# Two stacked transformer blocks on one core: ring slots, the order of splits and gates, and the PSUM banks of the last attentions rearranged

## The chip, the cores and the metric

The kernel runs on one core of a Trainium2 chip as one launch. The metric is the device time of that launch in microseconds (us), as the median of the runs shown. Times inside a run come from one execution that the hardware profiler recorded.

## The reference

The input `x` is 512 tokens of 1024 features in float32. Two blocks are computed one after the other. What matters of them, cut down:

```python
# block 1, two layers (l = 0, 1)
proj = h @ w_in[l]                         # q, k, v, gates of three kinds of attention
ya = differential_attention(...) * silu(ag)    # kind A: 4 heads, two maps each, rope on q and k
yb = forgetting_attention(...) * silu(bg)      # kind B: 4 heads
yc = stick_breaking_attention(...) * silu(cg)  # kind C: 4 heads
h = layernorm(ALPHA * h + concat(ya, yb, yc) @ w_out[l])
# block 2, one layer
proj = rms_norm(x) @ w_in_2
score = sum over 8 heads of relu(iq . ik) * iw # kind I; then the 128 largest of each row
o_a = attention over the chosen keys + bias    # kind X: 4 heads
o_b = hgrn2_mixer(q, f, i, g)                  # "hgrn": 4 heads, chunks of 64
o_c = mla_attention(...)                       # kind M: 4 heads
mixed = sigmoid(gates) * (o_a @ up_a, o_b @ up_b, o_c @ up_c), summed
x = x + mixed @ w_out_2
x = x + (silu(h @ w_ffn_gate) * (h @ w_ffn_up)) @ w_ffn_down
out = rms_norm(x)
```

## The kernel before, in words

A planner written in Python (`plan`, with `second` for block 2) makes one list of `steps`. Each of the five engines walks this same list and takes out of it what is its own, in order; semaphores join them. So the order of the list is the order in every engine's queue.

**Groups and split weights.** A `group` is one accumulation into one PSUM bank. The large ones multiply in three terms per slice of 128 features (x_high w_high, x_low w_high, x_high w_low), with K = 8 slices, so 24 matmuls for 512 columns. A weight piece (512 KB) is loaded by a transfer on SyncE's queue into a slot of the `raw` ring, ScalarE copies its rounded high part into a slot of the `high` ring (L1952), and GpSimd subtracts the high part from the raw piece in place (L1422). The step that does both is `split`; `place_splits` puts it behind the group that frees its slots (`free_raw`, `free_high`) and never ahead of the step named by `state["after"]`. The transfer of a piece waits for the last group that used what lay in its raw slot. The activations are split in the same way by `split_x`: ScalarE copies the high part (L1968), VectorE subtracts (L2422).

**Rings.** `RINGS_1` serves block 1 and the start of block 2 (7 raw slots, 7 high), `RINGS_FRONT` the projections around the I items (5 and 5), `RINGS_MIX` everything up to the end of the hgrn part (3 and 3), `RINGS_TAIL` the rest (9 and 9). A new ring starts again at its first slot. The plan's groups of block 1 and hgrn use three PSUM banks (`proj`) in turn; two banks hold scores, one the turned probabilities (`T`), two the outputs (`O[0]`, `O[1]`).

**Items.** An item is one head and one tile of 128 queries; it has K = 128 to 512 keys. `tick` emits one stage of each of several items: scores of item n, `soft1` of n, `soft2` of n-1, for kind C `soft3` of n-2, `trans` of n-3 (TensorE turns the probabilities into T, ScalarE copies T to SBUF, L1842), `pv` of n-4, and `fin` of a unit (all tiles of one head or pair) when its last item is 4 behind. For kind I the tick also emits two rounds of `topk` and one step of the list `tables` (20 entries: for each of four heads one `bias_rows` and four `bias` groups, the latter followed by two predicated copies on VectorE, L2122).

**Weaving.** In block 1 `weave` gives each projection job a weight; weight times a rate of the item kind is credit, and one tick is made per whole credit, for kinds B and C also in the middle of a group (a `half` step, then the rest). Before the output projection `wo` the groups of tiles 0 and 1 are begun on chunks 0 to 5 of y (`half`, `cut` = 6), then `flush` ticks the last items out, and the rest follows. In the hgrn part `paced` follows a written list of jobs per head: levels -1 to 5 (`hg_attn`), between them projections of the next head and `next_gate`, then `hg_turn`, `hg_state`, `hg_chain` (VectorE), `hg_out`, `hg_meansq`, `hg_norm`. `next_gate` emits `sig_min`, `sig_ln`, `sig_out` of earlier gates and one `sigmoid` group of 24 matmuls. ScalarE's copy of group i out of its bank (L1779) waits until the transfer of gate i-2 to DRAM has landed. There are 24 such gates; 22 come before the step `tail`, two behind it, and then the 24 `up` groups.

The `tail` step makes ScalarE wait for all scores, outputs and gates. `split_x` of y chunks writes into the buffer `hT_high`, which the projections read.

## Time and profile before

| | us |
|---|---|
| median of 3 runs | 1962.64 (1958.49 to 1964.73) |
| the profiled execution, time | 1960.21 |
| its span | 1958.4 |
| TensorE (PE) busy | 1747.6 |
| VectorE (DVE) busy | 866.7 |
| ScalarE (ACT) busy | 801.5 |
| GpSimd (POOL) busy | 590.6 |
| granted TensorE clock, mean | 0.94 |

Times in rows are us from the start of the span. In a row of a timeline the first number is the start, the second the duration of the merged instructions; in brackets stands how long the engine was idle before it and what ended that. A row of waits has the total, the number and the longest. A row of windows has the stretch, its length, then busy time and number of instructions of PE, PE's weight loads, DVE, ACT and POOL, then the granted TensorE clock (1.00 is 2.4 GHz, 0.50 is 1.2 GHz), the busy share of the DMA engines and GB/s. With a source line only that line's engine is counted. PE = TensorE, PEld its weight loads, SP = SyncE.

### The profile page before, as it was taken

Reading aid. Unit: us, or ns where it says so; the run is one execution under the profiler, and the core shown is the slowest. Engines: PE = TensorE matmul, PEld = TensorE weight load, DVE = VectorE, ACT = ScalarE, POOL = GpSimd, SP = SyncE. Lnnn points to the kernel's source line nnn. Section 1 sums busy time; section 2 is a strip of 40 time slices with the busy share of each in tenths; the row PEclk is TensorE's granted clock in tenths of the full one; section 3 lists DMA queues with packets and bytes.
Section 4 is the critical chain, followed back from the end, with each engine's and each line's share of the span. In section 5 each row is a group of like instructions: output and inputs, shape, how many; then the busy total and the mean of one; then the engine's idle time right before and its main releaser. Section 6 shows DMA issues by size and latency. Waiting matters only on the chain. (4 is left out here: it accounts for less than half of the span.)

```text
span 1958.4 us, 20995 instructions
## 1 busy us (share of the span) xinstructions
PE 1747.6 (89%) x7742; PEld 1325.8 (68%) x7742; DVE 866.7 (44%) x1478; ACT 801.5 (41%) x1512; POOL 590.6 (30%) x291
## 2 busy tenths in 40 slices
PE   4899998889999987898989898978779989999997
PEld 3666765567667655675655675767658778888786
DVE  4353344553533445452895656465417313211402
ACT  2244446522344465323324555555443334443411
POOL 4332222134322121322211222222046435444540
PEclk9998999899989998998989998989889989999999
DMA  6312212033122120323112222322155333333221
GB/s 179 92 44 65 65 44 65 12 86 87 46 65 57 51 75 12 87 81 87 32 46 65 60 70 60 113 60 74 39 168 187 86 95 97 97 96 99 77 97 43
DMA packets 204116, 149.85 MB, mean 77 GB/s; under 512 B 14956, under 2 KB 183536, under 8 KB 204016
## 3 DMA queue, kind: packets, MB, share of 16 engines
q1 hardware_dynamic: 199488, 133.57, 24.1%
q0 software_dynamic: 4528, 14.95, 2.4%
q8 instruction: 63, 1.03, 0.2%
q14 instruction: 37, 0.30, 0.0%
HBM read 138.00 MB, written 10.49 MB: 76 GB/s over the span
## 5 line engine op out<-in xcount | busy, mean ns | idle before, releaser
L1422 POOL TENSOR_TENSOR weights_rounded<-weights_raw,weights_rounded 128x1024 fp32r<-128x1024 f32 (+1 forms) x237 | 562.9, 2392 | 1153.1 <-ACT weights_rounded L1952 1152.8
L1488 PE MATMUL proj<-hT_high,weights_rounded 128*128 128x512 f32 (+1 forms) x1904 | 643.0, 409 | 35.7 <-POOL weights_rounded L1422 20.4
L1488 PEld LDWEIGHTS proj<-hT_high,weights_rounded 128*128 128x128 f32 x1904 | 370.1, 195 | 126.2 <-issue 39.0
L1488 PE MATMUL proj<-hT_low,weights_rounded 128*128 128x512 f32 (+1 forms) x952 | 379.1, 398 | 0.0
L1952 ACT ACTIVATE weights_rounded<-weights_raw 128x1024 fp32r<-128x1024 f32 (+1 forms) x237 | 233.6, 1009 | 140.2 <-DMA weights_raw<-in_w_ffn_down 58.7
L1484 PE MATMUL proj<-weights_rounded,hT_high 128*128 128x512 f32 (+1 forms) x640 | 209.3, 405 | 40.7 <-DVE hT_low L2033 15.8
L1488 PEld LDWEIGHTS proj<-hT_low,weights_rounded 128*128 128x128 f32 x952 | 185.7, 195 | 40.4 <-issue 5.3
L1484 PEld LDWEIGHTS proj<-weights_rounded,hT_high 128*128 128x128 f32 x640 | 125.9, 200 | 71.6 <-issue 32.2
L1611 PE MATMUL score<-qk 64*128 64x256 f32 (+3 forms) x256 | 79.6, 496 | 28.4 <-DVE logits L2201 15.2
L1654 PE MATMUL attn_out<-probs_T,V 128*64 128x128 f32 (+1 forms) x560 | 89.2, 294 | 0.0
L1640 PE MATMUL turned_probs<-constants,probs 128*128 128x128 f32 x320 | 61.0, 291 | 22.7 <-ACT probs_T L1842 22.5
L1654 PEld LDWEIGHTS attn_out<-probs_T,V 128*64 128x64 f32 (+1 forms) x560 | 69.6, 171 | 11.0 <-issue 9.3
L1484 PE MATMUL proj<-weights_rounded,hT_low 128*128 128x512 f32 (+1 forms) x192 | 74.2, 387 | 0.0
L1611 PEld LDWEIGHTS score<-qk 64*128 64x128 f32 x256 | 29.8, 194 | 62.4 <-issue 34.2
L2141 DVE TENSOR_REDUCE small<-score 128x1 f32<-128x128 f32 (+3 forms) x64 | 28.3, 484 | 91.3 <-PE score L1615 91.3
L1488 PE MATMUL score<-hT_high,weights_rounded 128*128 128x512 f32 (+2 forms) x208 | 66.1, 395 | 0.0
L1640 PEld LDWEIGHTS turned_probs<-constants,probs 128*128 128x128 f32 x320 | 37.2, 148 | 30.7 <-DVE probs L2179 18.4
L1814 ACT ACTIVATE E<-score,small 128x128 f32<-128x128 f32 (+3 forms) x64 | 33.2, 524 | 57.9 <-DVE small L2141 57.9
L1842 ACT ACTIVATE probs_T<-turned_probs 128x128 f32<-128x128 f32 (+3 forms) x128 | 54.3, 424 | 4.3 <-PE turned_probs L1640 4.3
L1690 ACT ACTIVATE tg<-proj 128x512 f32<-128x512 f32 x31 | 18.5, 596 | 91.6 <-PE proj L1488 91.5
L1817 ACT ACTIVATE E<-logits,small 128x128 f32<-128x128 f32 (+3 forms) x48 | 26.9, 560 | 70.1 <-DVE small L2161 70.0
L1733 ACT ACTIVATE qk<-proj 128x512 f32<-128x512 f32 x30 | 17.9, 598 | 90.4 <-PE proj L1488 90.4
(463 smaller groups left out, 2794.1 us busy)
## 6 DMA issues: line engine op xcount, KB each, us to landing
weights_raw<-in_w_in SPq DMA_DIRECT2D x113, 512.0 KB, 4.1
weights_raw<-in_w_out SPq DMA_DIRECT2D x24, 512.0 KB, 3.8
weights_raw<-in_w_ffn_gate SPq DMA_DIRECT2D x22, 512.0 KB, 3.9
weights_raw<-in_w_ffn_up SPq DMA_DIRECT2D x22, 512.0 KB, 3.8
weights_raw<-in_w_ffn_down SPq DMA_DIRECT2D x22, 512.0 KB, 3.6
gates<-constants POOLq DMA_DIRECT2D x24, 256.0 KB, 2.7
weights_raw<-gates SPq DMA_DIRECT2D x24, 256.0 KB, 4.9
weights_raw<-in_w_in SPq DMA_DIRECT2D x20, 256.0 KB, 3.2
```

Source lines behind the costliest of these rows:

```text
L1422: nc.gpsimd.tensor_tensor(piece_view(WR, p, "raw"), piece_view(WF, p, "raw"), piece_view(WR, p, "high"), ALU.subtract).then_inc(w_low, 1)
L1484: mm = nc.tensor.matmul(ps[:, 0:gr["N"]], x_[:, k, t * P:(t + 1) * P], w_[:, 0:gr["N"]], start=first, stop=last)
L1488: mm = nc.tensor.matmul(ps[:, on], w_[:, c0:c0 + P], x_[:, k, on], start=first, stop=last)
L1611: nc.tensor.matmul(ps[:, 0:K], qk[r, it["q"], tq], qk[r, it["k"], 0:K], start=True, stop=False)
L1640: mm = nc.tensor.transpose(T[:, j * P:(j + 1) * P], PR[:, i % 3, j * P:(j + 1) * P], cn("ident"))
L1654: mm = nc.tensor.matmul(O[u % 2][r0:r0 + rn, t * P:(t + 1) * P], v, PT[:, i % 2, j * P:(j + 1) * P], start=(j == 0), stop=(j == t))
L1690: link(nc.scalar.activation(dst, src, ACT.Abs, **kw))
L1814: ins = nc.scalar.activation(e[:, j, :], sc[(first_map[n] + j) % SCORE_BANKS][:, 0:K], ACT.Exp, bias=nmax[:, c + j:c + j + 1], accum_out=s ...
L1817: ins = nc.scalar.activation(e[:, 0, :], L[:, n % 2, 0:K], ACT.Exp, bias=nmax[:, c:c + 1], accum_out=sums[:, c:c + 1])
L1842: nc.scalar.activation(PT[:, i % 2, 0:it["K"]], T[:, 0:it["K"]], ACT.Copy).then_inc(turned_out, 1)
L1952: nc.scalar.activation(piece_view(WR, p, "high"), piece_view(WF, p, "raw"), ACT.Copy).then_inc(w_high, 1)
L2141: ins = nc.vector.tensor_reduce(nmax[:, c + j:c + j + 1], sc[(first_map[n] + j) % SCORE_BANKS][:, 0:K], AX, ALU.max, negate=True)
```

## The change

The edits, in the order of the diff:

1. `RINGS_1` gets one more slot behind the others in the bias region (8 raw, 7 high); the bias table's staging (`circulant`) moves to the buffer `gate_e`. `RINGS_FRONT` and `RINGS_TAIL` keep their slots but start at another one. 
2. For I items of the last tile `tick` takes two entries of `tables` instead of one.
3. In block 1 the first projection job of head 1 has weight 0 instead of 1, the second 1.6 instead of 1.1.
4. `split_x` of y chunks 0 to 4 moves from behind the last tick of the weave to between the group of the last gate (c = 5) and its `gate2`.
5. The `wo` group of tile 2 is begun before the `flush` too, with a tick ahead of it.
6. In hgrn a `next_gate` stands between `hg_turn` and `hg_state`; the one between `hg_meansq` and `hg_norm` (for the last head the one behind `hg_state`) is gone. For the last head the ticks are 2 behind `hg_out`.
7. `state["after"] = ("tail", 0)` moves behind the last two gates.
8. From the first M item on, turned probabilities alternate between T and `O[1]`, and all outputs of M and X items use `O[0]`.

```diff
-IN_POOL, IN_BIAS = [SLOT * i for i in range(POOL_SLOTS)], [BIAS_AT + SLOT * i for i in range(4)]
-RINGS_1 = IN_POOL[0:7], IN_POOL[7:10] + IN_BIAS
-RINGS_FRONT = IN_POOL[0:5], IN_POOL[5:10]
+IN_POOL, IN_BIAS = [SLOT * i for i in range(POOL_SLOTS)], [BIAS_AT + SLOT * i for i in range(5)]
+RINGS_1 = IN_POOL[0:8], IN_POOL[8:10] + IN_BIAS
+RINGS_FRONT = IN_POOL[4:5] + IN_POOL[0:4], IN_POOL[9:10] + IN_POOL[5:9]
...
-RINGS_TAIL = [PIECE * i for i in range(TAIL_RING)], [PIECE * (TAIL_RING + i) for i in range(TAIL_RING)]
+RINGS_TAIL = ([PIECE * i for i in (5, 6, 7, 8, 0, 1, 2, 3, 4)],
+              [PIECE * (TAIL_RING + i) for i in (2, 3, 4, 5, 6, 7, 8, 0, 1)])
...
-        if state["bias"] < len(tables) and n < len(items) and items[n]["kind"] == "I":
+        for _ in range(2 if n < len(items) and items[n]["tile"] == NT - 1 else 1):
+            if state["bias"] == len(tables) or n >= len(items) or items[n]["kind"] != "I":
+                break
...
-            jobs += [(lambda h=h: rope_raw(h, 0), 1, 0), (lambda h=h: rope_two(h), 1.1, 0),
+            jobs += [(lambda h=h: rope_raw(h, 0), int(h > 1), 0), (lambda h=h: rope_two(h), 1.1 + 0.5 * (h == 1), 0),
...
+            if c == 5:
+                for k in range(5):
+                    steps.append(("split_x", ("y", k, 1)))
             steps.append(("gate2", g))
...
-        for c in range(6):
-            steps.append(("split_x", ("y", c, 1)))
+        steps.append(("split_x", ("y", 5, 1)))
...
-        late.append(group("T", wo, N=512, K=KD, tile=1, dst=("resid", 0), src="y", layer=l, late=True))
-        steps.append(("half", late[1]))
-        groups[late[1]]["cut"] = 6
+        for t in (1, 2):
+            late.append(group("T", wo, N=512, K=KD, tile=t, dst=("resid", 0), src="y", layer=l, late=True))
+            steps.append(("half", late[t]))
+            groups[late[t]]["cut"] = 6
+            if t == 1:
+                tick()
         flush()
...
-        wide_tiles(wo, (2, 3), dst=("resid", 0), src="y", layer=l)
+        wide_tiles(wo, (3,), dst=("resid", 0), src="y", layer=l)
...
         jobs.append((lambda h=h: hgrn_turn(h), 1))
+        jobs.append((next_gate, 0))
         jobs.append((lambda h=h: hgrn_state(h), 1))
-        jobs.append((next_gate, int(last)))
-        jobs.append((lambda h=h: hgrn_out(h), int(last)))
+        if not last:
+            jobs.append((next_gate, 0))
+        jobs.append((lambda h=h: hgrn_out(h), 2 * last))
         if not last:
             jobs.append((next_gate, 0))
         jobs.append((lambda h=h: hgrn_meansq(h), int(last)))
-        if not last:
-            jobs.append((next_gate, 0))
         jobs.append((lambda h=h: hgrn_norm(h), 0))
     paced(jobs, its)
     flush()
-    state["after"] = ("tail", 0)
     steps.append(("tail", 0))
...
     new_rings(RINGS_TAIL)
+    state["after"] = ("tail", 0)
...
-        circulant = bias[:, 3, OFF[3]:OFF[4]].rearrange("p (h n) -> p h n", h=4)
+        circulant = gate_e[:, :].rearrange("p (h n) -> p h n", h=4)
...
+        first_pair = min((turned_at[n] - 1 for n, it in enumerate(items) if it["kind"] in "MX"), default=len(items))
+
+        def turned_bank(i):
+            return O[1] if i >= first_pair and (i - first_pair) % 2 else T
+
+        def out_bank(u):
+            return O[0] if units[u]["kind"] in "MX" else O[u % 2]
...
                     i = turned_at[arg] - 1
-                    if i:
+                    if i > first_pair:
+                        pe.wait_ge(turned_out, i - 1)
+                    elif i:
                         pe.wait_ge(turned_out, i)
+                    if i == first_pair + 1:
+                        for u in (it["unit"] - 2, it["unit"] - 1):
+                            unit_done(pe, u)
...
                     pe.wait_ge(turned_out, i + 1)
-                    if u >= 2:
+                    if it["kind"] in "MX":
+                        unit_done(pe, u - 1)
+                    elif u >= 2:
                         unit_done(pe, u - 2)
```

The transposes, their ScalarE copies, the `pv` matmuls and the `fin` copy take their bank from `turned_bank` and `out_bank`.

## Rows read from the trace of the kernel before

**Rows 1.** The page: the span and TensorE's busy time.
```profile
span 1958.4 us, 20995 instructions
PE 1747.6 (89%) x7742; PEld 1325.8 (68%) x7742; DVE 866.7 (44%) x1478; ACT 801.5 (41%) x1512; POOL 590.6 (30%) x291
```

**Rows 2.** TensorE's waits over the whole span.
```profile
PE turned_probs L1640 <- ACT probs_T L1842: 22.5, 18, 3.2
PE proj L1488 <- POOL weights_rounded L1422: 20.4, 2, 12.7
PE proj L1571 <- ACT qk L1781: 16.4, 4, 4.9
...
PE score L1611 <- DVE logits L2201: 15.2, 6, 5.5
PE proj L1484 <- DVE branches_low L2422: 13.3, 4, 5.1
...
PE proj L1484 <- POOL weights_rounded L1422: 8.7, 4, 3.8
PE score L1611 <- DVE qk L2027: 8.5, 2, 5.1
...
PE score L1620 <- ACT E L1825: 6.8, 2, 3.7
...
PE proj L1488 <- ACT tg L1697: 4.1, 2, 3.2
```

**Rows 3.** Windows: five stretches of granted clock 0.50.
```profile
83.26:90.09 6.83, 4.89 (x16) 3.83 (x17) 2.29 (x3) 1.41 (x5) 1.25 (x1) 0.50 0.01 3
...
407.50:410.90 3.40, 3.40 (x9) 2.61 (x9) 0.75 (x2) 0.00 (x0) 0.00 (x0) 0.50 0.03 7
895.60:905.90 10.30, 5.24 (x12) 4.12 (x13) 0.00 (x0) 5.78 (x6) 7.73 (x4) 0.50 0.90 223
...
1120.90:1131.20 10.30, 8.74 (x29) 5.54 (x30) 4.09 (x12) 4.83 (x11) 4.70 (x2) 0.50 0.00 0
...
1417.90:1431.50 13.60, 4.83 (x12) 3.79 (x13) 3.33 (x3) 4.30 (x6) 5.21 (x3) 0.50 0.05 20
```

**Rows 4.** Timeline of TensorE, layer 0: three waits in front of scores and of wo.
```profile
128.38 0.92 PE L1611 MATMUL score<-qk 64*128 64x384 f32 x4 [2.35 <-ACT E L1814]
...
320.76 0.79 PE L1611 MATMUL score<-qk 64*128 64x256 f32 x1 [5.54 <-DVE logits L2201]
...
350.76 0.76 PE L1484 MATMUL proj<-weights_rounded,hT_high 128*128 128x512 f32 x1 [5.10 <-DVE branches_low L2422]
```

**Rows 5.** Timeline of VectorE, layer 0: the low parts of y chunks 0 to 5.
```profile
349.92 3.70 DVE L2422 TENSOR_TENSOR branches_low<-y,hT_high 128x512 fp32r<-128x512 f32 x6 [0.18 <-ACT hT_high L1968]
```

**Rows 6.** Windows: VectorE before and during the topk rounds; last, line L2122 alone.
```profile
910.00:940.00 30.00, 30.00 (x104) 18.13 (x104) 8.06 (x14) 10.37 (x18) 0.60 (x1) 1.00 0.20 53
940.00:1030.00 90.00, 78.93 (x285) 52.27 (x284) 85.94 (x177) 28.32 (x55) 18.48 (x8) 0.94 0.17 43
...
946.50:1030.00 83.50, 16.34 (x20) 0.93 0.18 46
```

**Rows 7.** Timeline of TensorE: the first projection from a normalised latent.
```profile
1029.84 1.19 PE L1488 MATMUL proj<-probs,weights_raw 128*128 128x512 f32 x1 [4.31 <-issue]
```

**Rows 8.** ScalarE in the hgrn part: one copy of a gate, and all such waits.
```profile
1120.29 0.60 ACT L1779 ACTIVATE constants<-proj 128x512 f32<-128x512 f32 x1 [3.07 <-DMA gates<-constants]
...
ACT constants L1779 <- DMA gates<-constants: 68.6, 19, 5.1
```

**Rows 9.** Timeline behind the tail step: ScalarE's splits, then a wait of TensorE.
```profile
1423.01 1.99 ACT L1952 ACTIVATE weights_rounded<-weights_raw 128x1024 fp32r<-128x1024 f32 x2
...
1452.33 0.76 PE L1488 MATMUL score<-branches_high,weights_rounded 128*128 128x512 f32 x1 [3.39 <-POOL weights_rounded L1422]
```

**Rows 10.** Timeline of VectorE: a rope addition and the next product.
```profile
76.78 2.78 DVE L2027 TENSOR_TENSOR qk<-tg,raw 128x512 f32<-128x512 f32 x1
79.69 0.69 DVE L2024 TENSOR_TENSOR tg<-proj,constants 128x512 f32<-128x512 f32 x1
```

More of the change, by code:

```diff
@@ L1008, in two_blocks @@
         WR = over("weights_rounded", base, [P, (IN_BIAS[-1] + SLOT) // 4])
-        assert IN_BIAS[-1] + SLOT <= BIAS_AT + 4 * (3 * OFF[NT] + OFF[3])
+        assert IN_BIAS[-1] + SLOT <= BIAS_AT + 4 * (4 * OFF[NT] + S)
         WF = over("weights_raw", base, [P, (IN_BIAS[-1] + SLOT) // 4], F32)
@@ L1636, in _ @@
                     i = turned_at[arg] - 1
-                    if i:
+                    if i > first_pair:
+                        pe.wait_ge(turned_out, i - 1)
+                    elif i:
                         pe.wait_ge(turned_out, i)
+                    if i == first_pair + 1:
+                        for u in (it["unit"] - 2, it["unit"] - 1):
+                            unit_done(pe, u)
                     for j in range(it["tile"] + 1):
-                        mm = nc.tensor.transpose(T[:, j * P:(j + 1) * P], PR[:, i % 3, j * P:(j + 1) * P], cn("ident"))
+                        mm = nc.tensor.transpose(turned_bank(i)[:, j * P:(j + 1) * P], PR[:, i % 3, j * P:(j + 1) * P], cn("ident"))
                     mm.then_inc(turned, 1)
@@ L1653, in _ @@
                         v = avv[:, j, :] if it["kind"] == "X" else V[:, j, v0:v0 + vn]
-                        mm = nc.tensor.matmul(O[u % 2][r0:r0 + rn, t * P:(t + 1) * P], v,
+                        mm = nc.tensor.matmul(out_bank(u)[r0:r0 + rn, t * P:(t + 1) * P], v,
                                               PT[:, i % 2, j * P:(j + 1) * P], start=(j == 0), stop=(j == t))
@@ L1841, in _ @@
                         act.wait_ge(pv_done, i - 1)
-                    nc.scalar.activation(PT[:, i % 2, 0:it["K"]], T[:, 0:it["K"]], ACT.Copy).then_inc(turned_out, 1)
+                    nc.scalar.activation(PT[:, i % 2, 0:it["K"]], turned_bank(i)[:, 0:it["K"]], ACT.Copy).then_inc(turned_out, 1)
                 elif op == "fin":
@@ L1851, in _ @@
                         dst = oc if u["kind"] == "M" else y
-                        nc.scalar.activation(dst[:, u["chunk"], :], O[arg % 2][:, :], ACT.Copy).then_inc(o_free["other"], 1)
+                        nc.scalar.activation(dst[:, u["chunk"], :], out_bank(arg)[:, :], ACT.Copy).then_inc(o_free["other"], 1)
                 elif op == "fin2":
```

## The prediction, made before the changed kernel was run

> **What bounds the kernel now.** I read the page first: TensorE is busy for 1747.6 of 1958.4 us and the next engine for 866.7 [rows 1], so time is made by what TensorE waits for. Then the waits of TensorE: most of the long ones have one cause and come at the same place of each layer or head [rows 2]. Then windows around the waits, since a wait costs more than itself: behind each long one the granted clock is 0.50 (1.2 GHz) instead of 1.00 (2.4 GHz) for 3.4 to 13.6 us [rows 3]. Half of what TensorE is busy in such a stretch is lost. After a wait of 5.07 us that is 4.89 / 2 = 2.4 us, after the one in hgrn's state 8.74 / 2 = 4.4, behind `tail` 4.83 / 2 = 2.4. The third window, 3.40 us wholly busy, gives 1.7. Last I looked at whether VectorE or ScalarE would keep TensorE from using the time. That is so in one stretch, 940 to 1030, where VectorE is busy for 85.94 of 90 us [rows 6].
>
> The sum is made against the profiled execution's own 1960.2 us, which is 2.4 below the median of 1962.6; I add 2.4 at the end.
>
> **The change part by part.** No instruction is added or removed except semaphore waits; all is order, slots and banks. Each price is the wait plus half of the slow work behind it.
>
> *Weights 0 and 1.6 (edit 3).* The first scores of a layer wait for VectorE's rope, 8.5 us in two layers, the longer 5.1 [rows 2]. With weight 0 the tick comes one projection (24 matmuls, 5.6 us by their spacing in full-clock stretches) later, which covers it: 5.1 + 2.4 in layer 0, 3.4 + 1.7 in layer 1, 12.6 together. Followed through the job list, the credit then makes its first double tick at items 2 and 3 instead of 5 and 6; the double tick at 5 and 6 waited 2.35 us [rows 4], the new one has nothing between its scores and more keys, about 3.0. Two new double ticks, items 8 and 9 and 14 and 15, cost about 0.8 each. That is 2.2 back per layer, 4.4. And the phase of the credit removes a double tick: items 36 and 37 of kind C follow each other now, and the second waits 5.54 us for VectorE's logits [rows 4], which with the same in layer 1 and two short ones makes the 15.2 of [rows 2]. With half a gate (3.0 us) between them about 2.5 stays, so 3.0 + 2.4 (the slow half, by the first window of [rows 3]) less some slack, 5 per layer, 10. Sum 12.6 - 4.4 + 10 = 18; low 8, high 23.
>
> *Split of y ahead of gate2 (edit 4).* The half group of wo waits 5.10 us for the low parts [rows 4], which VectorE makes in 3.70 us for six, beginning at 349.92, behind gate2, gate3 and one item [rows 5]. Moved, the first low part is there some 3.5 us sooner, since ScalarE can copy as soon as its logarithm is out. But chunk 5 then comes behind gate2, gate3 and an item of 512 keys, and TensorE will wait there for most of what it won. I take 3 per layer, 6; low 2, high 13 (both waits and their slow halves gone). Late next is chunk 5.
>
> *Third half group (edit 5).* 18 matmuls move ahead of the flush. The flush ends in the chain of its last item, which they don't cover; they let ScalarE and VectorE empty their queues first. 2 per layer, 4; low 0, high 8. All three proj banks are then held through the flush, where nothing else wants one.
>
> *Eighth raw slot (edit 1).* The fourth piece of wo's second half is loaded only when the group before is done, since seven slots make it land where the first half lay; TensorE waits 3.81 and 3.44 us in the two layers, within the 8.7 of [rows 2]. With the eighth its slot is free four groups earlier; only ScalarE's and GpSimd's parts stay behind that group (3.5 us), and the third slice pair needs them after 18 matmuls (4.2 us). So 7.25 and two times 1.7: 10.6; low 8, high 12. The extra piece of 512 KB that now goes ahead of the constants at the start delays them by some 2 us of a slack of 20: nothing. Without that slack it would cost those 2.
>
> *First slot of RINGS_FRONT and two tables per tick (edits 1, 2).* The first piece of the new ring lands where the last projection's weights lie and is loaded after it: the shorter of the two in 20.4, so 7.7 us [rows 2], and 5.24 / 2 = 2.6 slow [rows 3]. Starting at the fifth slot the load can go four groups sooner and this wait goes. But VectorE's topk rounds follow, which begin when the eighth I item is through, and are followed back to back up to the latents; TensorE waits for them at 1001 and 1005 (6.8 [rows 2]) and 1029.84 (4.31 [rows 7]). So only what moves VectorE counts. It begins its rounds earlier by 10.3, less eight bias groups that now come before (7.4 us of TensorE) and a wait or so for a copy of `bias_rows` (1), that is 2 us; and another 1.5 since the short tables aren't behind it. Of its 16.34 us of predicated copies in 20 instructions [rows 6] 12 go to the time before, where it is busy for 8.06 of 30: 12 x 0.817 = 9.8, less 0.9 for a tighter queue. 2 + 1.5 + 8.9 = 12.4; low 6, high 16.
>
> *Gate between turn and state (edit 6).* `hg_state` waits for ScalarE's copy of the turned decay: 16.4 us in four heads [rows 2]. ScalarE is late because it stands at the copy of the gate before until a transfer to DRAM has landed, 3.07 us here, 68.6 in all [rows 8]. 5.6 us of gate on TensorE covers it. Slow halves as in the fourth window of [rows 3], and by the same rule 4.8, 2.8 and 3.3 for the other heads: 15.3. The copy that waited behind the gate removed ahead of `hg_norm` gives another 4.1 [rows 2] and 1.6 of slow work. That is 37. For the last head the gate no longer lies between item 151 and the flush, so I take 4 off. The ScalarE queue stays as blocked as it was, with two gates closer together, so a fourth of the rest may come back as waits for a bank: 33 x 0.75 = 25. Low 10, high 37.
>
> *Two banks for turned probabilities, one for outputs (edit 8).* Transposes wait for ScalarE's copy of the item before, 22.5 us in all, 10 of them from here on [rows 2]. With two banks the transposes go, but the next matmuls, `pv` of the item before, wait for the very same copy. So what is won is only the transposes' own time, 0.3 to 0.9 us at four places, and perhaps a slow stretch: 3; low -6, high 10. The single output bank makes `pv` of a new head wait for `fin` of the last; `fin` is in the tick before, with 3 to 6 us of other groups between.
>
> *Tail (edits 1, 7).* The weights of the last two gates are in SBUF long before but are split behind `tail`, at 1423.01 [rows 9], and TensorE waits 12.7 us [rows 2] plus 2.4. Then the first `up` pieces wait for the gates' own slots and for ScalarE, another 3.0 and 3.39 [rows 9]. With both moved the two gates run at once, the first three `up` pieces are split behind `tail` under the gates, and the fourth comes behind two gate copies that each wait for a transfer: some 3 stay. 15.1 + 6.4 + 1.7 (the slow stretch behind the last) less 3, less 2 for a queue of ScalarE that is as long as before: 18. Low 12, high 22.
>
> Sum: 18 + 6 + 4 + 10.6 + 12.4 + 25 + 3 + 18 = 97. Waits as yet hidden behind those removed will show; by the two that I could follow (chunk 5 and the fourth `up` piece, some 3 each) I take 7 off. 1960.2 - 90 = 1870.2, with 2.4 added 1872.6, say 1872.
>
> **A rule weighed.** A rope addition on VectorE takes 2.78 us while GpSimd splits weights, where its kind takes 0.69 [rows 10]. The first splits of a layer and the ak2 piece now come earlier, onto the rope and onto the angles. That the two clash is in the rows; the Trainium skill (SBUF — State Buffer, "SBUF: two separate sides") says that an addition with both inputs in SBUF and a GpSimd operation exclude each other for their whole length. By that rule it speaks against the early splits; it is the second rival below.
>
> **The rivals.**
> *A: the stall is handed on.* TensorE's waits turn into others of the same queue, ScalarE standing at gate copies. For it: 68.6 us of such waits [rows 8] stay; against: the new covers are longer than the lateness seen. Then hgrn gives 10, the tail 12, the halves 0 and the weights 12: 2 + 0 + 10.6 + 12.4 + 10 + 0 + 12 + 12 = 59, so 1903 to 1905.
> *B: VectorE stretched by GpSimd.* Ten additions or more of the critical ones at 2.1 us each lose 21, and the rope covers (edit 3) half of their 18: 97 - 30 - 7 = 60, again 1902. For it: POOL's pieces move by whole groups; against: POOL is busy 30% only.
> *C: all waits go.* The terms' highs are 23 + 13 + 8 + 12 + 16 + 37 + 10 + 22 = 141: 1822; with the hidden waits, some 120: 1842.
> *D: slower.* The single output bank: if each of the seven head changes of M and X had `pv` behind a `fin` that ScalarE reaches only after a gate transfer, queue and slow clock, it would have to cost 13 us each to eat 90. The longest wait of ScalarE for that transfer is 5.1 [rows 8], so it needs more than twice that.
> *E: no change.* Two repairs work and the rest is absorbed by one chain. I see none of that length outside 940 to 1030.
>
> **How the numbers follow.** The likeliest, 1848 to 1895: 0.60. A or B, 1895 to 1925: 0.20. C, 1815 to 1848: 0.14. Something between there and 1957: 0.02. E 0.01, D 0.03. The range 1845 to 1912 holds the likeliest, most of A and B and the edge of C, about 0.8. What this kernel's measurement can tell from no change is 0.3%, 6 us. Faster 0.96, same 0.01, slower 0.03.
>
> **What would show it.** TensorE's busy time little less than before but its waits about 60 to 70 us less, clock mean up. Right: no wait in front of the first scores, of wo's seventh slice and of the ak2 group; the waits <-ACT qk gone; last two gates without a gap behind item 151; topk starting about 3 us nearer to item 96 and ending 12 nearer. Wrong: waits <-ACT turned_probs now at `pv` are half or less of before (the banks are worth more than I say); a wait for chunk 5 missing (edit 4 is worth more) or over 4 us; waits for `gates` copies in front of projections (A); VectorE's rope operations at 2 to 3 us in number (B). The prediction fails most easily in hgrn, where taking 25 of the 37 is my judgement and not a row.

## The result and the profile after

The changed kernel takes 1907.8 us (median of 4 runs, 1905.3 to 1912.7) against 1961.5 of the kernel before, run beside it. The ratio is 0.9729 with a 95% interval of 0.9703 to 0.9754: 53 us faster. Forecast were 1872 as the likeliest time and 1845 to 1912 as the range, so the time lies near the range's slow end, outside the likeliest band (1848 to 1895, given 0.60) and in the one of the rivals A and B (1895 to 1925, given 0.20): 54 us won where 90 were expected.

The page of the changed kernel, to be read beside [rows 1]:

```profile
span 1903.5 us, 20988 instructions
PE 1727.7 (91%) x7742; PEld 1312.7 (69%) x7742; DVE 867.4 (46%) x1478; ACT 799.3 (42%) x1512; POOL 594.5 (31%) x291
```

Of the 54.9 us by which the span is shorter, 19.9 are TensorE's busy time (less work at the slow clock) and 35 are waits. Its waits by what ended them, to be read beside [rows 2]:

```profile
PE proj L1500 <- DVE branches_low L2445: 16.7, 6, 4.6
...
PE turned_probs L1661 <- ACT probs_T L1865: 13.3, 14, 1.5
...
PE proj L1504 <- ACT constants L1802: 11.6, 6, 3.0
PE score L1627 <- ACT E L1837: 10.1, 6, 3.4
PE score L1627 <- DVE logits L2224: 8.4, 6, 2.6
PE attn_out L1677 <- ACT probs_T L1865: 8.4, 4, 2.8
PE proj L1504 <- POOL weights_rounded L1438: 7.9, 4, 2.2
PE turned_probs L1504 <- POOL weights_rounded L1438: 7.1, 1, 7.1
...
```

Gone are the waits of the state for ScalarE's copy (16.4), those of the first scores (8.5) and of 12.7 and 7.7 for weights. But five groups are new or larger: y's low parts 16.7 (13.3 before), scores for ScalarE's exponentials 10.1 (4.7), copies of gates 11.6 (4.7), 7.1 for an `up` piece (3.4), and four waits for pieces among the I items, 7.9 together.

To see where the 54.9 were won I took, in both traces, the start of the same matmul at places where TensorE has done the same work, and subtracted. The third column is what has been won up to there. Of the names, aq is the first query projection of a head of kind A, to_hT a transpose of the activations at the start of block 2, ak2 the first projection of `RINGS_FRONT`, hf a gate projection of hgrn, and wo2 the output projection of block 2.

```
place                                         before    after    won
block 1, layer 0: aq of head 1                 74.10    73.82    0.3
  item 30 (scores)                            282.59   282.72   -0.1
  item 36 (scores)                            313.99   314.16   -0.2
  wo, first half, tile 3                      393.78   393.92   -0.1
  wo, second half, tile 2                     415.82   410.24    5.6
layer 1: aq of head 1                         469.81   461.78    8.0
  item 78 (= 30)                              675.62   668.40    7.2
  wo, first half, tile 3                      786.44   779.59    6.9
  wo, second half, tile 2                     808.12   795.91   12.2
block 2: to_hT of tile 2                      839.85   827.89   12.0
  last I item (scores)                       1005.89   984.09   21.8
  hf of head 0                               1016.93   996.20   20.7
  hgrn, last head's mean square              1410.57  1370.03   40.5
  wo2, tile 1                                1525.62  1470.71   54.9
```

Read down, a rise is what a stretch has won. By this reading edits 3, 4 and 5 together won nothing in layer 0, and little in layer 1. The eighth slot won 5.7 and 5.4 (from tile 3 of wo's first half to tile 2 of its second), which leaves 0.9 of the 12.0 for the three edits. The front part up to hf of head 0 won 8.8, the hgrn part with the banks 19.8, the tail 14.4.

### The profile page after: what moved, and what is told of

The parts are those of the page before. It is cut to its first block and busy times, and to the rows that moved or that the text cites. A ratio compares the mean times of both kernels' runs of the same rounds, so it can differ in the third digit from the quotient of the medians.

```text
span 1903.5 us, 20988 instructions
## 1 busy us (share of the span) xinstructions
PE 1727.7 (91%) x7742; PEld 1312.7 (69%) x7742; DVE 867.4 (46%) x1478; ACT 799.3 (42%) x1512; POOL 594.5 (31%) x291
## 3 DMA queue, kind: packets, MB, share of 16 engines
q1 hardware_dynamic: 199488, 133.57, 24.6%
## 5 line engine op out<-in xcount | busy, mean ns | idle before, releaser
L1438 POOL TENSOR_TENSOR weights_rounded<-weights_raw,weights_rounded 128x1024 fp32r<-128x1024 f32 (+1 forms) x237 | 567.0, 2408 | 1154.7 <-ACT weights_rounded L1975 1154.5
L1504 PE MATMUL proj<-hT_high,weights_rounded 128*128 128x512 f32 (+1 forms) x1904 | 641.7, 409 | 25.9 <-ACT constants L1802 11.6
L1500 PE MATMUL proj<-weights_rounded,hT_high 128*128 128x512 f32 (+1 forms) x640 | 203.6, 395 | 34.8 <-DVE branches_low L2445 16.7
L1627 PE MATMUL score<-qk 64*128 64x256 f32 (+3 forms) x256 | 81.7, 507 | 18.6 <-ACT E L1837 10.1
L1677 PEld LDWEIGHTS attn_out<-probs_T,V 128*64 128x64 f32 (+1 forms) x560 | 67.2, 166 | 15.2 <-issue 9.0
L1661 PE MATMUL turned_probs<-constants,probs 128*128 128x128 f32 x272 | 51.7, 289 | 13.3 <-ACT probs_T L1865 13.3
L2072 DVE SCALAR_TENSOR_TENSOR tg<-proj,tg 128x512 f32<-128x512 f32 x20 | 13.8, 692 | 91.2 <-ACT tg L1715 91.2
L1500 PE MATMUL proj<-weights_rounded,branches_low 128*128 128x512 f32 x128 | 51.0, 398 | 0.0
```

The lines of the kernel that those rows point to most:

```text
L1438: nc.gpsimd.tensor_tensor(piece_view(WR, p, "raw"), piece_view(WF, p, "raw"), piece_view(WR, p, "high"), ALU.subtract).then_inc(w_low, 1)
L1500: mm = nc.tensor.matmul(ps[:, 0:gr["N"]], x_[:, k, t * P:(t + 1) * P], w_[:, 0:gr["N"]], start=first, stop=last)
L1504: mm = nc.tensor.matmul(ps[:, on], w_[:, c0:c0 + P], x_[:, k, on], start=first, stop=last)
L1627: nc.tensor.matmul(ps[:, 0:K], qk[r, it["q"], tq], qk[r, it["k"], 0:K], start=True, stop=False)
L1661: mm = nc.tensor.transpose(turned_bank(i)[:, j * P:(j + 1) * P], PR[:, i % 3, j * P:(j + 1) * P], cn("ident"))
L1677: mm = nc.tensor.matmul(out_bank(u)[r0:r0 + rn, t * P:(t + 1) * P], v, PT[:, i % 2, j * P:(j + 1) * P], start=(j == 0), stop=(j == t))
```

## The experiments

Unless it says otherwise, each starts from the changed kernel. The ratio is that to the kernel before, run beside it, where the changed kernel has 0.9729 [0.9703, 0.9754]. The kernel before took 1962.6 us beside the runs without edit 3, 4, 6 and 8, 1959.8 beside those without edits 3, 4 and 5, with one table and the last two rows, and 1960.7 beside the others. The ratios allow for that; a difference of two medians below can be off by 1 or 2 us from it alone.

```
edit                                      median    ratio  [95% interval]
3 undone (weights of head 1)             1900.6    0.9690 [0.9667, 0.9712]
4 undone (split of y)                    1905.1    0.9710 [0.9687, 0.9733]
3, 4 and 5 undone                        1908.4    0.9737 [0.9722, 0.9751]
6 undone (gates of hgrn)                 1926.0    0.9825 [0.9804, 0.9846]
8 undone (banks)                         1908.7    0.9732 [0.9713, 0.9752]
tail of edits 1 and 7 undone             1918.6    0.9781 [0.9748, 0.9814]
start of RINGS_FRONT undone              1907.3    0.9735 [0.9714, 0.9755]
one table per tick (edit 2 undone)       1910.6    0.9747 [0.9732, 0.9762]
other raw slots in RINGS_TAIL            1897.7    0.9683 [0.9665, 0.9700]
GpSimd's subtraction in halves           1900.0    0.9688 [0.9661, 0.9714]
the last two, and 3 undone               1883.5    0.9609 [0.9593, 0.9625]
the same with weights 0 and 1.9          1887.0    0.9624 [0.9610, 0.9638]
```

**Edit 3 undone.**

```diff
-(lambda h=h: rope_raw(h, 0), int(h > 1), 0), (lambda h=h: rope_two(h), 1.1 + 0.5 * (h == 1), 0)
+(lambda h=h: rope_raw(h, 0), 1, 0), (lambda h=h: rope_two(h), 1.1, 0)
```

> The changed kernel with the job weights of head 1 back at 1 and 1.1. By the prediction's sum (edit 3 worth 18) it takes 1907.8 + 18 = 1926, with the waits of 5.1 and 3.4 us in front of the first scores, of 2.35 at item 6 and of 5.5 at item 37 back. The rival, from a comparison of both traces at places where TensorE has done the same work: up to item 30 of a layer edit 3 won nothing in layer 0 and 2.0 in layer 1, because the new double tick of items 2 and 3 waits 3.39 us itself, so it takes 1908 to 1912. A third theory, that one rope product of 9.46 us on VectorE in layer 0, which ends only with the fifth of GpSimd's weight subtractions in a row, took what the weights gave: then no DVE operation of 9 us is in this trace where scores come earlier, and layer 1 (where none is long) loses more by the undoing than layer 0.

It is 7 us faster than the changed kernel. So this edit, forecast to win 18, costs. The two intervals overlap by a hair (0.9712 and 0.9703); the traces bear the loss out. The table's places say where: up to item 36 the two kernels are alike (each loses 0.4 in layer 0, 0.2 and 0.8 in layer 1), but from there to the last group of wo's first half this one wins 4.2 and 3.7 us against before, and the changed one nothing. TensorE's waits in that stretch of layer 0, first in the changed kernel, where the fourth comes at the chunk-5 matmuls:

```profile
320.94 0.70 PE L1627 MATMUL score<-qk 64*128 64x256 f32 x2 [2.58 <-DVE logits L2224]
...
333.57 1.12 PE L1627 MATMUL score<-qk 64*128 64x512 f32 x2 [1.18 <-DVE logits L2224]
...
343.93 0.47 PE L1500 MATMUL proj<-weights_rounded,hT_high 128*128 128x512 f32 x1 [2.26 <-DVE branches_low L2445]
...
352.15 0.50 PE L1500 MATMUL proj<-weights_rounded,hT_high 128*128 128x512 f32 x1 [4.57 <-DVE branches_low L2445]
```

and with the old weights:

```profile
322.34 1.22 PE L1627 MATMUL score<-qk 64*128 64x256 f32 x2 [5.54 <-DVE logits L2224]
...
341.23 0.49 PE L1627 MATMUL score<-qk 64*128 64x128 f32 x2 [1.61 <-DVE logits L2224]
...
348.83 0.47 PE L1500 MATMUL proj<-weights_rounded,hT_high 128*128 128x512 f32 x1 [1.72 <-DVE branches_low L2445]
...
354.06 0.50 PE L1500 MATMUL proj<-weights_rounded,hT_high 128*128 128x512 f32 x1 [1.55 <-DVE branches_low L2445]
```

10.59 us of waits against 10.42: the 5.54 became 2.58 as forecast, and came back in front of wo. With the new weights item 41 is no longer done before the half group of wo, so this begins 3.5 us earlier, counted from item 36, and VectorE isn't ready for it. And the 4 us? The windows from item 36 to tile 3 of wo, both layers, changed kernel first:

```profile
314.20:393.90 79.70, 64.24 (x276) 43.13 (x276) 41.45 (x59) 42.33 (x89) 9.44 (x4) 0.89 0.07 20
699.80:779.60 79.80, 64.34 (x277) 43.25 (x277) 41.44 (x59) 42.33 (x89) 9.45 (x4) 0.89 0.07 20
```

```profile
315.60:391.20 75.60, 59.94 (x277) 40.95 (x277) 40.27 (x59) 42.25 (x89) 9.52 (x4) 0.93 0.06 21
697.80:773.50 75.70, 60.09 (x277) 41.03 (x277) 40.25 (x59) 42.23 (x89) 9.53 (x4) 0.93 0.07 21
```

TensorE is idle for 15.5 and 15.7 us, and busy for 64.2 against 59.9 with the same matmuls: the whole difference is slow clock (0.89 against 0.93). These are two traces, but others say the same. Seven kernels, the changed one among them, have one and the same plan for block 1. Of their 14 stretches from item 36 to tile 3 of wo 12 take 79.2 to 79.8 us and 2 take 75.7. With the old weights all four take 74.3 to 75.7 (two here, two in the run of all that helped, which has the halved subtraction too; with the new weights and halves they are 77.1 and 78.8). The third theory falls: the long rope product is there too (8.71 us in layer 0).

**Edit 4 undone.** The edit moves the five lines back: `for c in range(6): steps.append(("split_x", ("y", c, 1)))` behind the last tick.

> The changed kernel with all six low parts of y back behind the last tick. By the prediction (edit 4 worth 6, one wait of about 5 us in front of wo instead of one of 3 for chunk 5) 1914. The rival, from the trace after, where TensorE waits 2.26 us for chunk 0 and 4.57 for chunk 5 in either layer, 13.7 together, and 10.2 before: the edit lost, and without it the kernel takes 1902 to 1907, with one wait of about 5 us in front of the seventh slice's half group in each layer.

1905.1, 2.6 faster, which the intervals don't tell from no change. One wait of 6.96 us takes the place of 2.26 and 4.57:

```profile
345.39 0.76 PE L1498 MATMUL proj<-weights_rounded,hT_high 128*128 128x512 f32 x1 [6.96 <-DVE branches_low L2443]
```

Part of the 4.57 in the changed kernel is GpSimd's: the low part of chunk 5 takes 2.07 us on VectorE, the five before it 3.09 together.

```profile
343.10 3.09 DVE L2445 TENSOR_TENSOR branches_low<-y,hT_high 128x512 fp32r<-128x512 f32 x5
...
350.02 2.07 DVE L2445 TENSOR_TENSOR branches_low<-y,hT_high 128x512 fp32r<-128x512 f32 x1
```

With the new weights the split in front of `gate2` saves 0.1 us of waits a layer; with the old ones it turned 5.10 [rows 4] into 1.72 and 1.55 (the run above), which is 1.8 a layer.

**Edits 3, 4 and 5 undone.**

> The changed kernel with edits 3, 4 and 5 undone, only the eighth raw slot kept in block 1. By the prediction's terms (18 + 6 + 4) 1936. By what the runs so far give: 1900.6 without edit 3, and in that trace edits 4 and 5 win 4.2 and 3.7 us between item 36 and the last wo group of the first half in the two layers, so 1908 to 1909, the time of the changed kernel: the three edits together are worth nothing. In front of the wo half group a wait of about 5.1 us in each layer.

1908.4, as the second theory says. The three edits together are worth 0.7 us, with one interval inside the other; without edit 3 the other two are worth 7.8 (1908.4 less 1900.6). Edit 5 was not undone alone. Of edits 1 to 5 this kernel keeps in block 1 only the eighth slot, and in its trace the same two stretches of wo win 5.7 and 5.3 us, as in the changed kernel.

**Edit 6 undone.** The gates stand again as in the kernel before.

> The changed kernel with the gates of the hgrn part in the old order. By the prediction (25) 1933; if it was worth the whole 37, 1945; by the comparison of traces (19.9 won from the first head's projections to the last head's mean square, of which 1 to 3 are the banks') 1925 to 1928. The four waits of the state for ScalarE's copy come back with 3.6 to 4.9 us each, and the waits of gates for their bank, 11.6 us after, fall to about 5. If the waits of gates stay at 10 or more, they weren't the price of this edit.

It costs 18.3. The waits between 1030 and 1420, without the edit and then with it:

```profile
PE proj L1587 <- ACT qk L1804: 17.0, 4, 4.8
...
PE proj L1504 <- ACT tg L1720: 8.2, 2, 7.4
PE proj L1504 <- ACT constants L1802: 4.9, 3, 2.1
```

```profile
PE proj L1504 <- ACT constants L1802: 11.6, 6, 3.0
...
PE proj L1596 <- ACT constants L1802: 2.6, 1, 2.6
PE proj L1540 <- ACT tg L1810: 2.1, 1, 2.1
```

25.2 us of waits are removed and 6.7 for banks of gates, 2.6 for the output's bank and 1.7 for the mean square (2.1 less the 0.4 without the edit) come for them: 14.2 net. The rest of the 18.3 I put down to the slow clock (mean granted 0.945 in this trace, 0.955 with the edit); it was not counted out stretch by stretch. The copies of gates that hold a bank stand behind their transfer, 76.5 us in all on ScalarE (71.3 before; 68.6 in [rows 8] was for 19 of them):

```profile
ACT constants L1802 <- DMA gates<-constants: 76.5, 22, 6.3
```

**Edit 8 undone.** `first_pair = len(items)`, and `out_bank` returns `O[u % 2]`.

> The changed kernel with one bank for turned probabilities and two for outputs everywhere. By the prediction (3) 1911: the four waits of pv for ScalarE's copy (1.4, 2.4, 2.8 and 1.9 us after) turn back into waits of the transposes, each longer by 0.3 to 0.6 us. If two banks were worth more than their own transposes' time, 1915 or above. If the single output bank cost something (the rival that would have made the change slower), the kernel is faster without: 1900 to 1905.

1908.7: nothing that can be measured. In the hgrn part the transposes wait 11.5 us in five, where with two banks `pv` waits 8.4 in four: 3.1 us of waits as forecast, of which 0.9 shows in the medians. The rival by which the single output bank costs 13 us a head is out: no wait for `fin` is in the trace.

```profile
PE turned_probs L1661 <- ACT probs_T L1863: 11.5, 5, 3.7
```

**The tail undone.** `RINGS_TAIL` in its old order and `state["after"]` ahead of `tail`.

> The changed kernel with the splits of the last two gates' weights behind the tail step again and the last ring in its old order. By the prediction (18) 1926; by the comparison of traces, which shows 13.8 won between the last head's mean square and the sixth up group because a wait of 7.05 us stays in front of the fourth, 1921 to 1922, with a wait of some 12.7 us behind the last item back.

1918.6, with a wide interval: 10.9 us by the medians. In its trace the whole span wins 41.3 instead of 55.0, which is 13.7; from the last head's mean square to the end it loses 1.7 us against the kernel before, where the changed one wins 14.5. The wait of 12.7 is back:

```profile
PE proj L1503 <- POOL weights_rounded L1437: 12.7, 1, 12.7
```

**The start of RINGS_FRONT undone.** `IN_POOL[0:5], IN_POOL[5:10]`.

> The changed kernel with RINGS_FRONT starting at its first slot again, two tables per tick kept. By the prediction the wait of 7.7 us in front of the ak2 group comes back but only what moves VectorE's topk rounds counts, 2 of the 12.4: 1910. The rival: the stretch is set by TensorE and every us counts, 7.7 and 2.6 of slow clock: 1918.

**One table per tick.** `for _ in range(1):`.

> The changed kernel with one table entry per tick of I items, the front ring's new start kept. By the prediction 10.4 of the 12.4 of this stretch go with it: 1918. The rival: the topk rounds aren't what sets the end of the stretch and the copies cost the same wherever they stand: 1908 to 1911. VectorE's busy time between 940 and 1030 should rise to about 86 of 90 us again, and the last topk step end some 10 us later, if the prediction's step is right.

These two belong together. Undone alone, the ring costs nothing (1907.3) and the tables 2.8 us (1910.6), neither clear of noise. No run undoes both. From to_hT of tile 2 to the last I item the changed kernel wins 9.8 us, the one without the new start 7.9 (from 15.5 to 23.4), the one with one table 7.8 (from 7.9 to 15.7). So each alone gives 8 of the 10, and the second adds only 2. Up to hf of head 0, where the changed kernel has won 8.8, it is 5.5 without the new start and 7.8 with one table.

The ring's old start does not bring the old wait back. The prediction and the expectation had 7.7 us in front of the ak2 group; the trace has 2.78:

```profile
879.68 0.77 PE L1504 MATMUL proj<-hT_high,weights_rounded 128*128 128x512 f32 x1 [2.78 <-POOL weights_rounded L1438]
```

So 5 of the 7.7 us had gone by another edit. The eighth raw slot is the likely one, since it too changes where the pieces lie, but no run shows it. With one table the ak2 group doesn't wait, but items 118 and 119 do, 8.1 us:

```profile
PE score L1636 <- ACT E L1848: 8.1, 2, 5.0
```

VectorE was busy for 81.39 of the 90 us from 940 on in that kernel and 81.29 in the changed one (85.94 in [rows 6]); the 86 that I expected there didn't come. Nor did two tables shorten the topk rounds: from the first topk instruction to the last they take 103.8 us in the changed kernel and 102.8 before, though 12 predicated copies moved ahead of them.

**Other raw slots in RINGS_TAIL.**

```diff
-RINGS_TAIL = ([PIECE * i for i in (5, 6, 7, 8, 0, 1, 2, 3, 4)],
+RINGS_TAIL = ([PIECE * i for i in (5, 6, 7, 3, 4, 8, 0, 1, 2)],
```

> The changed kernel with another order of raw slots in RINGS_TAIL: the fourth and fifth up piece take slots that are free before the last gates, so that ScalarE can split them behind the tail step and not behind two gate copies that each wait for a transfer. If these copies are what the wait of 7.05 us in front of the fourth up group is for, it goes with its slow half: 1899 to 1902. The rival: the sixth piece waits in the same queue of ScalarE and TensorE waits for it 5.8 us later instead, and little is won: 1905 to 1908.

In the changed kernel ScalarE stands for 6.26 us at the copy of the second gate behind the tail, and only then splits the fourth piece:

```profile
1382.38 1.66 ACT L1975 ACTIVATE weights_rounded<-weights_raw 128x512 fp32r<-128x512 f32 x3
1385.59 0.60 ACT L1802 ACTIVATE constants<-proj 128x512 f32<-128x512 f32 x1 [1.55 <-DMA gates<-constants]
...
1394.96 0.60 ACT L1802 ACTIVATE constants<-proj 128x512 f32<-128x512 f32 x1 [6.26 <-DMA gates<-constants]
...
1397.97 1.13 ACT L1975 ACTIVATE weights_rounded<-weights_raw 128x512 fp32r<-128x512 f32 x2
```

```profile
1400.45 0.77 PE L1504 MATMUL turned_probs<-branches_high,weights_rounded 128*128 128x512 f32 x1 [7.05 <-POOL weights_rounded L1438]
```

With the other slots five pieces are split ahead of both copies, and TensorE's next wait is 0.55 us for the sixth:

```profile
1385.47 2.70 ACT L1975 ACTIVATE weights_rounded<-weights_raw 128x512 fp32r<-128x512 f32 x5
```

```profile
1402.46 0.47 PE L1504 MATMUL attn_out<-branches_high,weights_rounded 128*128 128x512 f32 x1 [0.55 <-POOL weights_rounded L1438]
```

1897.7, 10.1 faster, with intervals apart. The first theory holds.

**GpSimd's subtraction in halves.** Each low part of a weight piece as two instructions:

```diff
-nc.gpsimd.tensor_tensor(piece_view(WR, p, "raw"), piece_view(WF, p, "raw"),
-                        piece_view(WR, p, "high"), ALU.subtract).then_inc(w_low, 1)
+cut = raw_w.shape[-1] // 2
+nc.gpsimd.tensor_tensor(raw_w[..., 0:cut], raw_f[..., 0:cut], high_w[..., 0:cut], ALU.subtract)
+nc.gpsimd.tensor_tensor(raw_w[..., cut:2 * cut], raw_f[..., cut:2 * cut], high_w[..., cut:2 * cut],
+                        ALU.subtract).then_inc(w_low, 1)
```

> The changed kernel with each of GpSimd's 237 weight subtractions made as two instructions of half the columns. If a SBUF to SBUF operation of VectorE waits for the GpSimd instruction that runs, the 82 stretched VectorE operations (125.7 us over their shortest durations) lose about half of that, the one of 9.46 us in layer 0 falls below 3, and the kernel is faster by 2 to 8 us: 1900 to 1906. The rival: VectorE is let in only when GpSimd's queue has a gap, as in the 9.46 us, so two halves in a row hold it as long as one whole: the excess stays over 110 and the time stays or grows by GpSimd's extra instructions, 1908 to 1913.

The time is 7.8 us lower, but the intervals of this run and of the changed kernel overlap a little (up to 0.9714 and from 0.9703). The next run bears out this gain and that of edit 3 undone together, 14.2 us more than the other slots alone give; it does not tell the two apart. Both theories are partly right. At the rope of layer 1, in the changed kernel and then with halves, the blocked addition and product lose about 1.1 us each:

```profile
462.81 2.78 DVE L2050 TENSOR_TENSOR qk<-tg,raw 128x512 f32<-128x512 f32 x1
...
466.34 2.07 DVE L2048 TENSOR_TENSOR raw<-raw,constants 128x512 f32<-128x512 f32 x1
```

```profile
463.55 1.67 DVE L2054 TENSOR_TENSOR qk<-tg,raw 128x512 f32<-128x512 f32 x1
...
465.96 0.97 DVE L2052 TENSOR_TENSOR raw<-raw,constants 128x512 f32<-128x512 f32 x1
```

Yet the long product of layer 0 became longer, 10.10 us, over eight of GpSimd's instructions. Summed over all VectorE operations that take over 0.2 us more than the shortest of their line and shape, the excess fell from 125.7 us in 82 to 100.4 in 108, not to half. GpSimd's own busy time rose from 567.0 to 627.8:

```profile
L1441 POOL TENSOR_TENSOR weights_rounded<-weights_raw,weights_rounded 128x512 fp32r<-128x512 f32 (+1 forms) x237 | 318.7, 1345 | 1101.9 <-ACT weights_rounded L1979 1101.5
L1442 POOL TENSOR_TENSOR weights_rounded<-weights_raw,weights_rounded 128x512 fp32r<-128x512 f32 (+1 forms) x237 | 309.1, 1304 | 0.0
```

**All that helped, together.** Edit 3 undone, the other slots and the halves.

> Three things at once on the changed kernel: job weights of head 1 back at 1 and 1.1 (7 us by its own run), the other order of raw slots in the last ring (10 us), GpSimd's subtraction in two halves (8 us). They act in block 1, in the tail and at VectorE's operations under GpSimd everywhere; if they add up, 1883, and if the halves' gain was partly the waits that the others remove, 1885 to 1890.

1883.5. The three gains, 7.1, 10.1 and 7.8, give 1882.8: they add up, within 1 or 2 us. It is 4% faster than the kernel before and 1.2% faster than the changed one.

**The same with weights 0 and 1.9.**

> As the kernel before it in this list, but with the weights 0 and 1.9 instead of 1 and 1.1: the first scores come one projection later, and item 41 is still done before wo's half group. The theory that the phase of the credit is what cost the change (item 41 came behind the half group, which then began 7 us too early for VectorE) says that the waits for y's low parts stay near 1.7 and 1.6 us as with the old weights, and that the later first scores win 3 to 6 us: 1878 to 1882. The rival: double ticks 0 and 1, and 40 and 41, wait about 3 and 5 us and eat it: 1884 to 1890.

1887.0, 3.5 slower than with 1 and 1.1. The waits for y's low parts fell to 3.1 us (9.7 with the old weights), more than I had said. But the double tick at items 40 and 41 has nothing between, and the waits for logits are 25.3 instead of 15.2, the longest 8.5:

```profile
PE score L1631 <- DVE logits L2228: 25.3, 8, 8.5
```

The rival holds. With all three pairs of weights tried (1 and 1.1, 0 and 1.6, 0 and 1.9) the lateness of VectorE and ScalarE in kind C is paid somewhere.

## Why the prediction was right in sign and some 35 us too hopeful

**Edits 3, 4 and 5: 28 forecast, 0.9 measured.** This is the step that failed, 27 of the 42.5 us by which the terms together fell short. It failed in four places. (1) "Two double ticks cost about 3.0 and 0.8": the new one at items 2 and 3 waits 3.39, that at 14 and 15 1.42, and the first scores' wait of 5.07 left 2.00 behind in front of layer 0's swap. Up to item 36 of either layer the edit changes nothing beyond 1 us. (2) "With half a gate between them about 2.5 stays": true, 2.58. But I priced this as a gain and didn't follow it to the next place where TensorE needs VectorE. Followed there, the same phase of the credit puts item 41 behind the half group. (3) For edit 4 "I take 3 per layer" was between two bounds, and chunk 5 took all. Its wait was 4.57 in this trace. In five of the six other kernels with this plan it was 2.93 to 2.98, so "some 3" was right for most; but with the 2.26 in front of chunk 0 that is 5.2 us, against the single 5.10 of the kernel before. (4) The slow clock was a fixed half behind each wait in my sum; here equal waits at other places cost 4.3 us more of it in each layer. I had named both late parties, and added the terms as if they didn't meet.

**Eighth raw slot: 10.6 forecast, 11.1 measured** by the places; both waits are gone. No run took it away, but the one that keeps it alone in block 1 wins the same. It also did what the sum gave to another edit: most of the wait for ak2 had gone before the front ring's new start (2.78 us left), if the reading above is right.

**Front ring and tables: 12.4 forecast, 8.8 measured** up to the first hgrn projections. The size was nearly right and its split wrong: "only what moves VectorE counts" gave the ring 2 and the tables 10.4, where either alone gives 8 up to the last I item. The ring's price rested on a wait of 7.7 us, and with the old start only 2.78 of it is there. The sign that I had named, topk "starting about 3 us nearer to item 96 and ending 12 nearer", did not come: item 96 comes 24.6 us earlier than before (at 884.1), the first topk round 21.6 and the last 20.6, so that they lie 3.0 and 4.0 us farther from it. That the sum of this term is near is partly luck.

**Gate order and banks: 25 and 3 forecast, 18.3 and 0.9 by the runs, 19.8 together by the places.** The mechanism was right, all four waits of the state are gone. The size was off: I let a fourth of 33 come back as waits for banks, and of 25.2 us of waits 11.0 came back. The banks did what was said, moved the waits to `pv`.

**Tail: 18 forecast, 14.4 by the places, 10.9 by the run.** The step "the fourth comes behind two gate copies that each wait for a transfer: some 3 stay" was right in place and wrong in size: 7.05 stayed, since ScalarE stood for 6.26 us until the second transfer had landed. Another order of slots took it away.

**Hidden waits: 7 taken off.** They were far too few. The shortfalls above are 27.1 + 3.6 + 8.2 + 3.6, less 0.5 for the slots and less these 7: 35.0, the difference between 90 and 54.9 up to rounding. The range held for another reason than the working: it was wide enough for most of A and B. The measured time lies 4 us inside it.

Of the rivals, A (the stall handed on) is what happened in block 1 and partly in hgrn; its terms had 12 for the weights and nothing for the halves, still too much. B (VectorE stretched by GpSimd) is real, but not new: the excess is 127.8 us in 85 operations before and 125.7 in 82 after. D, E and C are out.

## What to carry to other kernels

When a repair changes the phase of a planner's credit, follow every later item to the next place where both engines meet, and price two edits on one chain together. A wait is won only if the engine that was late is early at its next meeting. Here 11.0 of 25.2 us of waits came back in hgrn, and nearly all in block 1. Before a queue's instruction waits for a transfer, put ahead of it what other engines need; that took away the wait of 7.05 us by one line. When an edit is priced by a wait of the old trace, ask whether another edit of the same change removes it already, as with the front ring.

## What the runs showed of the hardware that was not expected

**VectorE can be passed over.** In layer 0 of the changed kernel a product of two operands in SBUF takes 9.46 us, where the same one takes 0.68 eleven us later:

```profile
73.53 0.69 DVE L2047 TENSOR_TENSOR tg<-proj,constants 128x512 f32<-128x512 f32 x1 [8.29 <-PE proj L1510]
74.14 9.46 DVE L2048 TENSOR_TENSOR raw<-raw,constants 128x512 f32<-128x512 f32 x1
...
85.06 0.68 DVE L2048 TENSOR_TENSOR raw<-raw,constants 128x512 f32<-128x512 f32 x1
```

GpSimd, held for 4.99 us by a transfer, works off five subtractions meanwhile:

```profile
70.43 0.80 POOL L1406 DMA_DIRECT2D gate_logs<-bias_table  x1 [4.99 <-DMA bias_table<-logits]
71.25 11.79 POOL L1438 TENSOR_TENSOR weights_rounded<-weights_raw,weights_rounded 128x1024 fp32r<-128x1024 f32 x5
```

The product ends 0.55 us after the last of them. The kernel before has such a queue too (held for 4.68 us, then six subtractions in 15.43), and there the same product takes 2.33, so the full queue alone doesn't decide it. Every one of the 82 stretched operations of this kernel, and of the 85 before, overlaps a subtraction of GpSimd. None of the 82 reads PSUM. The first row above, which does, takes 0.69 us during a subtraction; none of the 19 of its kind takes longer, and four of them begin during one. This agrees with the Trainium skill (SBUF — State Buffer, "SBUF: two separate sides"), by which the one that comes second waits for the other's whole instruction. But by the page it would wait for one instruction, and here it waited until four had ended, with halves until eight. It is so in all 13 kernels with eight raw slots (8.7 to 10.1 us each), and not in the kernel before, where VectorE and GpSimd took turns [rows 10]. Why VectorE gets its turn in one case and not in the other is open.

**The slow stretch of the clock falls differently.** In layer 0 of the kernel without the ring's new start the plan and the first wait (2.26) are those of the changed kernel, but the one for chunk 5 is 2.95 instead of 4.57, and from item 36 to tile 3 of wo 4.1 us are won instead of 0.1. Chunk 5's first matmul comes 8.22 us behind the start of the half group in both. What differs is where the granted clock is 0.5. In the ten us behind the wait for chunk 5 it is 0.54 in the changed kernel (first row) and 1.00 in the other (second row); there TensorE does part of the half group at 0.50 instead, and so waits less for chunk 5.

```profile
352.00:362.00 10.00, 9.85 (x30) 5.90 (x31) 4.57 (x10) 4.33 (x10) 0.00 (x0) 0.54 0.01 2
```

```profile
352.00:362.00 10.00, 9.50 (x44) 6.07 (x43) 3.72 (x7) 4.22 (x10) 0.00 (x0) 1.00 0.01 2
```

Single places of two traces can therefore differ by 4 us with no edit between them. In layer 1 both kernels win nothing there (-0.4 and 0.1). What edit 3 costs rests on the medians and on all 18 stretches told under "Edit 3 undone", not on this one.
